# Causal masks and their identity in rounded fp32 instead of bf16, in a hybrid attention and state-space block on one core

## The chip, the cores and the metric

The program runs on one core of a Trainium2 chip. The metric is the device time of one execution in microseconds (us). TensorE is called PE here, and its weight loads, which overlap with its matmuls, are counted apart as PEld; DVE is VectorE, ACT is ScalarE, POOL is GpSimd and SP is SyncE.

## What is computed

One layer of a streaming encoder over 256 tokens of width 2048, in fp32. The part that matters here is the mixer: forgetting attention with 16 heads, and a Mamba-2 state-space mixer (SSD) with 16 heads. Both need an exponent that is cut off by a causal mask:

```python
    c = jnp.cumsum(log_f, axis=1).transpose(0, 2, 1)
    s = s + cb[..., :, None] - c[..., None, :]
    mask = k_pos[None, :] <= q_pos[:, None]
    s = jnp.where(mask[None, None], s, -jnp.inf)
    pr = jax.nn.softmax(s, axis=-1)
...
    seg = a_cum[:, :, :, None, :] - a_cum[:, :, None, :, :]
    decay = jnp.exp(jnp.where(causal[None, None, :, :, None], seg, -jnp.inf))
```

Ahead of the mixer stands the product with `w_in`. After it come `w_out`, a gated convolutional feed-forward part (`w_gate_up`, `w_down`), a gate with per-layer embeddings, and a last RMS norm.

## The kernel before

**Weights.** All weight matrices pass through a ring of four chunks of 128x1024 fp32. SP loads a chunk, ACT writes its rounded part `w_hi` (L312, fp32r, which is rounded fp32), DVE writes the rest `w_lo` (L317), and PE multiplies: hi times hi, hi times lo, lo times hi. In the front part of the kernel these are L332, L333 and L334 (128 weight columns, 256 moving columns, 8 triples to a chunk), for the value groups L372 to L374 (512 moving columns), in the feed-forward part L344 and L346.

**Order of the work.** `plan()` fixes by hand after which chunk each side step of the mixer is issued, on PE at chunk n and on ACT and DVE at chunk n + LEAD (3 later). So PE's stream is: a chunk of weights, one step of a head, a chunk of weights, and so on. The SSD heads come at about 140 to 207 us, the attention heads at about 219 to 292 us.

**The exponent of a head** is built in PSUM by `exponent_terms` (L761): one fp32r matmul with 64 rows of weights and 384 moving columns (L764) spreads a head's row of cumulated sums, `ssd_row` or `fox_row`, over the partitions. Then two matmuls (L767) with the identity `ident_bf` as weights and a mask of 128x128 as moving operand add 0 or -1e30 to the two blocks on the diagonal, at columns 0 and 256 of the bank. `ssd` calls it at L831 with `mask_s`, as the whole step of the new head behind the older head's four matmuls (L821); `fox` calls it at L811 with `mask_q`, after the older heads' transposes (L778) and products (L791) and the scores of the new head (L806, L808). The last L767 signals `e_ready` or `s_ready`: ACT's exponential L1080 waits for the first, DVE's row maximum L1425 for the second. Behind L1425 on DVE stands the scaling of the head before (L1432), and PE's transposes L778 wait for that.

**Where the masks come from.** POOL clears `ident`, four small tiles, `mask_q` and `mask_s` (L590 to L596), waits for them, and selects 1 on the diagonal of `ident` (L598). PE and ACT wait for `consts_made` at 4, which comes at L599. The masks are selected behind that (L609, L610), then two key tiles are cleared (L614), and only then are the two loads of the 16-column pieces of `w_in` issued on POOL's queue (L618, L619). DVE makes `ident_bf` from `ident` in `make_row(1)` (L1388), between the steps that make `fox_row`.

Of the kernel before, what the change touches and what calls it, by code (L numbers as in the profile page):

```python
# [26 lines left out]
F32R = mybir.dt.float32r  # L27
BF16 = mybir.dt.bfloat16
ALU = mybir.AluOpType
# [3 lines left out]
P = 128  # L33
EPS = 1e-6
MASKED = -1e30
# [10 lines left out]
def build(nc, x, p, mix_norm_w, w_in, fox_forget_bias, ssd_conv_w, ssd_conv_b, ssd_dt_bias, ssd_A_log,  # L46
          ssd_D, ssd_norm_w, w_out, ffn_norm_w, w_gate_up, ffn_conv_w, ffn_conv_b, w_down, ple_norm_w,
          w_ple_gate, w_ple_proj, final_norm_w, out):
    _, T, D = x.shape
# [73 lines left out]
    with ctx:  # L123
# [3 lines left out]
        def sem(name):  # L127
            return ctx.enter_context(nc.semaphore(name))
# [6 lines left out]
        ident = sb("ident", [P, P])  # L135
# [15 lines left out]
        def at(name, shape, dt=F32, offset=None):  # L151
            size = 4 if dt != BF16 else 2
            for n in shape[1:]:
                size *= n
            offset = top[0] if offset is None else offset
            top[0] = max(top[0], (offset + size + 31) // 32 * 32)
            assert arena + top[0] <= nc.sbuf_usable_end, (name, arena + top[0], nc.sbuf_usable_end)
            return nc.alloc_sbuf_tensor_at(name, shape, dt, offset=arena + offset)

        K1 = 1024  # L160
# [23 lines left out]
        ssd_row, fox_row = at("ssd_row", [4 * H, 3 * P], F32R), at("fox_row", [4 * H, 3 * P], F32R)  # L184
        sel = at("sel", [P, 2 * H], F32R)
        sel_f = at("sel_f", [P, 2 * H])
        ident_bf = at("ident_bf", [P, P], BF16)
        mask_q, mask_s = at("mask_q", [P, P], BF16), at("mask_s", [P, P], BF16)
        dt_tok = at("dt_tok", [P, TT, 2 * H])
        ncum_tok = at("ncum_tok", [P, TT, 2 * H])  # L190
        d_all = at("d_all", [P, H])
# [1 line left out]
        row_sum = at("row_sum", [P, H, TT])  # L193
        row_inv = at("row_inv", [P, H, TT])
        y_sum = at("y_sum", [P, T])
        y_rms = at("y_rms", [P, T])
        fdc = at("fdc", [2 * H, 4])
        xtok = at("xtok", [P, TT, D], offset=40 * K1)
        x_squares, x_ssq = at("x_squares", [P, D], offset=0), at("x_ssq", [P, TT], offset=61 * K1)
# [26 lines left out]
        ps = ctx.enter_context(nc.psum_tensor("ps", [P, 8, 512], F32))  # L226
# [20 lines left out]
        pool_step, consts_made, masks_made = sem("pool_step"), sem("consts_made"), sem("masks_made")  # L247
# [326 lines left out]
        @block.gpsimd  # L574
        def _(pool):
            steps = [0]

            def link(ins):
                steps[0] += 1
                ins.then_inc(pool_step, 1)  # L580

            def linked():
                pool.wait_ge(pool_step, steps[0])

            def select(dst, src, keep, fill, base, per_partition, per_column, n):
                return pool.affine_select(out=dst, in_=src, compare_op=keep, fill=fill, base=base,
                                          pattern=[[per_column, n]], channel_multiplier=per_partition)

            pool.memset(fdc[:, 2:3], 0.0).then_inc(consts_made, 1)
            link(pool.memset(ident[:, :], 0.0))  # L590
            link(pool.memset(sel_f[:, :], 0.0))
            link(pool.memset(fdc[:, 1:2], -1.0))
            link(pool.memset(fdw[:, 0, :], 1.0))
            link(pool.memset(mask_q[:, :], 0.0))
            link(pool.memset(mask_s[:, :], 0.0))
            pool.memset(eps[:, :], EPS).then_inc(consts_made, 1)  # L596
            linked()
            select(ident[:, :], ident[:, :], ALU.not_equal, 1.0, 0, 1, -1, P).then_inc(consts_made, 1)  # L598
            pool.memset(ones[:, :], 1.0).then_inc(consts_made, 1)  # L599

            link(select(sel_f[:, :], sel_f[:, :], ALU.not_equal, 1.0, 0, 1, -1, 2 * H))
            linked()
            select(sel_f[:, :], sel_f[:, :], ALU.not_equal, 1.0, -2 * H, 1, -1, 2 * H).then_inc(masks_made, 1)

            select(fdc[:, 1:2], fdc[:, 1:2], ALU.is_ge, 1.0, H - 1, -1, 0, 1).then_inc(masks_made, 1)

            select(fdw[:, 0, P:P + 1], fdw[:, 0, P:P + 1], ALU.is_ge, 0.0, H - 1, -1, 0, 1).then_inc(masks_made, 1)

            select(mask_q[:, :], mask_q[:, :], ALU.is_ge, MASKED, 0, 1, -1, P).then_inc(masks_made, 1)  # L609
            select(mask_s[:, :], mask_s[:, :], ALU.is_ge, MASKED, 0, -1, 1, P).then_inc(masks_made, 1)  # L610
            pool.wait_ge(masks_made, 5)
            for i, half in enumerate((kE[P // 2:P, :, :], kO[0:P // 2, :, :], conv_in[:, :, 0:4])):

                pool.memset(half, 0.0).then_inc(masks_made, 1)  # L614
                pool.wait_ge(masks_made, 6 + i)

            with nc.allow_non_contiguous_dma(reason="the forget and dt columns of w_in are 16 wide"):
                pool.dma_start(w_fd[:, :, 0:H], win_v[:, :, c_f:c_f + H]).then_inc(fd_landed, 16)  # L618
                pool.dma_start(w_fd[:, :, H:2 * H], win_v[:, :, c_dt:c_dt + H]).then_inc(fd_landed, 16)  # L619

            for norm in range(1, 3):
                if norm == 1:

                    pool.wait_ge(a_exp, 1)
                    select(fdc[:, 3:4], fdc[:, 3:4], ALU.is_ge, 1.0, -H, 1, 0, 1).then_inc(a_ready, 1)

                    for b in range(WT // 2):
                        pool.wait_ge(gated, b // 2 + 1)
                        pair = xsT[:, 2 * b:2 * b + 2, :]
                        if b > 0:  # L630
                            linked()
                        link(pool.tensor_tensor(sq[:, :, :] if b > 0 else sumsq[:, :, :], pair, pair, ALU.mult))
                        if b > 0:
                            linked()
                            link(pool.tensor_tensor(sumsq[:, :, :], sumsq[:, :, :], sq[:, :, :], ALU.add))
                    linked()
                    pool.tensor_tensor(sumsq[:, 0, :], sumsq[:, 0, :], sumsq[:, 1, :], ALU.add).then_inc(y_squared, 1)
                for b in range(KD // 2):
                    pool.wait_ge(x_new, norm * (KD // 2) + b + 1)
                    if b == 0:  # L640
                        pool.wait_ge(y_sums_made, 1)
                        if norm > 1:
                            pool.wait_ge(sums_made, norm - 1)
                    pair = xT[:, 2 * b:2 * b + 2, :]
                    if b == 0:
                        link(pool.tensor_tensor(sumsq[:, :, :], pair, pair, ALU.mult))
                        continue
                    linked()
                    link(pool.tensor_tensor(sq[:, :, :], pair, pair, ALU.mult))
                    linked()  # L650
                    link(pool.tensor_tensor(sumsq[:, :, :], sumsq[:, :, :], sq[:, :, :], ALU.add))
                linked()
                pool.tensor_tensor(sumsq[:, 0, :], sumsq[:, 0, :], sumsq[:, 1, :], ALU.add).then_inc(squares_made, 1)
# [3 lines left out]
        def _(pe):  # L657
# [103 lines left out]
            def exponent_terms(bank, j, row, mask, start):  # L761

                both = 4 * H
                pe.matmul(ps[:, bank, 0:3 * P], sel[0:both, j:j + 1].to_broadcast([both, P]), row[:, :],  # L764
                          start=start, stop=False, skip_group_check=True)
                for dst in (0, T):
                    mm = pe.matmul(ps[:, bank, dst:dst + P], ident_bf[:, :], mask[:, :],  # L767
                                   start=False, stop=True, skip_group_check=True)
                return mm

# [169 lines left out]
            for n, (g, c) in enumerate(tail):  # L940
                i = n // GROUP
# [297 lines left out]
        def _(dve):  # L1239
# [101 lines left out]
            def link(ins):  # L1341
                fd_count[0] += 1
                ins.then_inc(fd_step, 1)
                dve.wait_ge(fd_step, fd_count[0])
# [35 lines left out]
            def make_row(attention):  # L1380
                n, c = 2 * H, fdr(1)
                src = fdw[:, 2 + 2 * attention:4 + 2 * attention, :].rearrange("h a t -> h (a t)")[:, 0:3 * P]
                if attention:

                    dst = fox_row
                    link(dve.tensor_scalar(src[:, 0:P], c[:, 0:P], -1.0, None, ALU.mult))
                    link(dve.tensor_scalar(src[:, P:3 * P], c, -1.0, None, ALU.mult))
                    dve.tensor_copy(ident_bf[:, :], ident[:, :])  # L1388
                else:


                    dst = ssd_row
                    link(dve.tensor_copy(src[:, 0:P], c[:, 0:P]))
                    link(dve.tensor_scalar(src[:, P:T], c[:, P:T], c[:, P - 1:P], None, ALU.add))
                    link(dve.tensor_copy(src[:, T:3 * P], c[:, P:T]))
                    dve.tensor_copy(sel[:, :], sel_f[:, :])
                link(dve.tensor_copy(dst[0:n, :], src))
                dve.tensor_tensor(dst[n:2 * n, :], src, dst[0:n, :], ALU.subtract).then_inc(cum_ready, 1)
# [336 lines left out]
```

## Time and profile before

| | |
|---|---|
| median of 3 runs | 1259.81 us (1259.72 to 1260.19) |
| the profiled execution | 1260.43 us, its span 1258.7 us |
| busy in the span: PE, PEld | 1245.7 us (99%), 1108.7 us (88%) |
| DVE, ACT, POOL | 856.7 us (68%), 616.9 us (49%), 60.8 us (5%) |
| mean granted clock of TensorE | 0.998 of full speed |
| moved by DMA | 226.94 MB, 180 GB/s on average |

The span goes from the first to the last instruction. A matmul's record begins where it is issued to the array and contains its way through it, so that successive records overlap: what PE's time is made of is read from start to start, not from durations.

### The profile page before, as it was taken

The numbers are of one execution on the slowest core, as the hardware profiler recorded it, in microseconds if no ns is written. First come the engines' busy times: TensorE is split into PE (matmuls) and PEld (weight loads), VectorE is DVE, ScalarE is ACT, GpSimd is POOL, SyncE is SP. The second block draws the span as 40 slices with busy tenths as digits, with TensorE's granted clock in tenths as the row PEclk, the third lists the DMA queues.
The fourth block names the chain that finished last, engine by engine and source line by source line (L and its number), as shares of the span: only waits on it lengthen the run. The fifth ranks groups of instructions, "written<-read, shape, count | busy, mean of one in ns | idle before, by whom it ended". The sixth has DMA issues, their size and how long they took to land.

```text
span 1258.7 us, 21432 instructions
## 1 busy us (share of the span) xinstructions
PE 1245.7 (99%) x7838; PEld 1108.7 (88%) x7838; DVE 856.7 (68%) x1120; ACT 616.9 (49%) x810; POOL 60.8 (5%) x66
## 2 busy tenths in 40 slices
PE   8999999999999999999999999999999999999997
PEld 7999998789999888888888888888888888888885
DVE  6698777677678776767767677676746464646554
ACT  6544555656444454444444454454444344444555
POOL 2000000001213100000000000000001010101000
PEclk9999999999999999999999999999999999999999
DMA  8566555344656666666666666666665656566652
GB/s 256 168 183 184 157 146 155 114 114 125 199 172 203 186 193 186 185 196 183 191 193 185 194 187 187 194 187 188 191 190 166 216 160 217 164 212 202 198 185 101
DMA packets 165885, 226.94 MB, mean 180 GB/s; under 512 B 10209, under 2 KB 101381, under 8 KB 165701
## 3 DMA queue, kind: packets, MB, share of 16 engines
q1 hardware_dynamic: 165732, 225.90, 59.3%
q8 instruction: 38, 0.62, 0.2%
q0 software_dynamic: 96, 0.26, 0.1%
q14 instruction: 19, 0.15, 0.0%
HBM read 224.03 MB, written 2.10 MB: 180 GB/s over the span
## 4 chain that ended last, share of the span: by engine, by line
PE 97%; DVE 1%; DMA 1%; ACT 0%; SPq 0%; issue 0%; ACTq 0%; DVEq 0%
PE ps L344 39%; PE ps L346 19%; PE ps L332 8%; PE ps L333 8%; PE ps L334 8%; PE ps L372 4%; PE ps L374 4%; PE ps L373 3%; DMA w_raw<-in_w_in 1%; PE ps L764 1%; PE ps L767 1%; PE ps L808 1%; DVE h_parts L1243 0%; PE ps L791 0%; PE ps L821 0%; PE ps L778 0%
## 5 line engine op out<-in xcount | busy, mean ns | idle before, releaser
L317 DVE TENSOR_TENSOR w_lo<-w_raw,w_hi 128x1024 fp32r<-128x1024 f32 x413 | 505.9, 1230 | 318.2 <-ACT w_hi L312 317.5
L312 ACT ACTIVATE w_hi<-w_raw 128x1024 fp32r<-128x1024 f32 x413 | 435.9, 1059 | 459.4 <-PE ps L346 341.2
L344 PE MATMUL ps<-h_parts,w_hi 128*128 128x512 f32 x1408 | 488.6, 394 | 0.0
L346 PE MATMUL ps<-h_parts,w_lo 128*128 128x256 f32 x1408 | 390.2, 277 | 0.0
L344 PEld LDWEIGHTS ps<-h_parts,w_hi 128*128 128x128 f32 x1408 | 264.0, 188 | 61.5
L346 PEld LDWEIGHTS ps<-h_parts,w_lo 128*128 128x128 f32 x1408 | 264.2, 188 | 0.0
L344 PE MATMUL ps<-act_parts,w_hi 128*128 (+1 forms) x704 | 244.4, 392 | 0.0
L346 PE MATMUL ps<-act_parts,w_lo 128*128 (+1 forms) x704 | 196.8, 280 | 0.0
L332 PE MATMUL ps<-h_parts,w_hi 128*128 128x256 f32 x576 | 165.8, 288 | 0.6 <-DVE w_lo L317 0.6
L333 PE MATMUL ps<-h_parts,w_hi 128*128 128x256 f32 x576 | 162.9, 283 | 0.0
L334 PE MATMUL ps<-h_parts,w_lo 128*128 128x256 f32 x576 | 162.9, 283 | 0.0
L344 PEld LDWEIGHTS ps<-act_parts,w_hi 128*128 128x128 f32 x704 | 132.1, 188 | 29.5 <-issue 0.4
L346 PEld LDWEIGHTS ps<-act_parts,w_lo 128*128 128x128 f32 x704 | 132.2, 188 | 0.0
L332 PEld LDWEIGHTS ps<-h_parts,w_hi 128*128 128x128 f32 x576 | 110.2, 191 | 1.4 <-issue 1.3
L333 PEld LDWEIGHTS ps<-h_parts,w_hi 128*128 128x128 f32 x576 | 110.4, 192 | 0.0
L334 PEld LDWEIGHTS ps<-h_parts,w_lo 128*128 128x128 f32 x576 | 110.2, 191 | 0.0
L332 PE MATMUL ps<-mixHi,w_hi 128*128 128x256 f32 x256 | 71.8, 280 | 0.0
L334 PE MATMUL ps<-mixHi,w_lo 128*128 128x256 f32 x256 | 71.6, 280 | 0.0
L333 PE MATMUL ps<-mixLo,w_hi 128*128 128x256 f32 x256 | 71.6, 280 | 0.0
L372 PE MATMUL ps<-w_hi,h_parts 128*128 128x512 f32 x168 | 67.0, 399 | 0.6 <-DVE w_lo L317 0.6
L374 PE MATMUL ps<-w_hi,h_parts 128*128 128x512 f32 x168 | 65.8, 392 | 0.0
L373 PE MATMUL ps<-w_lo,h_parts 128*128 128x512 f32 x168 | 65.4, 389 | 0.0
(248 smaller groups left out, 1115.3 us busy)
## 6 DMA issues: line engine op xcount, KB each, us to landing
w_raw<-in_w_gate_up SPq DMA_DIRECT2D x352, 256.0 KB, 3.2
w_raw<-in_w_in SPq DMA_DIRECT2D x88, 512.0 KB, 3.7
w_raw<-in_w_down SPq DMA_DIRECT2D x88, 512.0 KB, 4.6
w_raw<-in_w_out SPq DMA_DIRECT2D x32, 512.0 KB, 4.6
w_raw<-in_w_ple_gate SPq DMA_DIRECT2D x32, 512.0 KB, 4.6
w_raw<-in_w_ple_proj SPq DMA_DIRECT2D x4, 512.0 KB, 5.3
out_x<-out_tok SPq DMA_DIRECT2D x8, 256.0 KB, 2.9
xtok<-in_x SPq DMA_DIRECT2D x3, 512.0 KB, 9.1
```

The lines of the kernel that those rows point to most:

```text
L312: act.activation(parts(n)[0], w_raw[:, n % RING, :], ACT.Copy).then_inc(w_hi_made, 1)
L317: dve.tensor_tensor(lo, w_raw[:, n % RING, :], hi, ALU.subtract).then_inc(w_lo_made, 1)
L332: pe.matmul(dst, hi, opHi(k), start=start and m % 2 == 0, stop=False, skip_group_check=True)
L333: pe.matmul(dst, hi, opLo(k), start=False, stop=False, skip_group_check=True)
L334: mm = pe.matmul(dst, lo, opHi(k), start=False, stop=stop, skip_group_check=True)
L344: pe.matmul(ps[:, bank_of[m], :], hi, both.rearrange("p b t -> p (b t)"), start=first and k == 0, stop=False, skip_group_check=True)
L346: mm = pe.matmul(ps[:, bank_of[m], T:2 * T], lo, both[:, 0, :], start=False, stop=last and k == 1, skip_group_check=True)
L372: pe.matmul(dst, a, hi, start=first and kk == 0, stop=False)
L373: pe.matmul(dst, a, lo, start=False, stop=False)
L374: mm = pe.matmul(dst, b, hi, start=False, stop=last and kk == 1)
L764: pe.matmul(ps[:, bank, 0:3 * P], sel[0:both, j:j + 1].to_broadcast([both, P]), row[:, :], start=start, stop=False, skip_group_check=True)
L767: mm = pe.matmul(ps[:, bank, dst:dst + P], ident_bf[:, :], mask[:, :], start=False, stop=True, skip_group_check=True)
```

## The change

`ident_bf`, `mask_q` and `mask_s` are no longer bf16 but fp32r, and the identity is now called `ident_r`. An fp32r tile is written rounded, so POOL makes the masks in two fp32 tiles, `mask_qf` and `mask_sf`, which lie in bytes 30 K to 31 K of the arena (where `y_part` lies later), and DVE copies both into the fp32r tiles in `make_row(1)`, right behind the identity. The three tiles grow by 256 bytes each per partition. `y_rms` gets the memory of `y_sum`. The two matmuls L767 stay as they are, but for the type of their operands.

```diff
-        ident_bf = at("ident_bf", [P, P], BF16)
-        mask_q, mask_s = at("mask_q", [P, P], BF16), at("mask_s", [P, P], BF16)
+        ident_r = at("ident_r", [P, P], F32R)
+        mask_q, mask_s = at("mask_q", [P, P], F32R), at("mask_s", [P, P], F32R)
+        mask_qf, mask_sf = (at(n, [P, P], offset=30 * K1 + 512 * i) for i, n in enumerate(("mask_qf", "mask_sf")))
...
-        y_rms = at("y_rms", [P, T])
+        y_rms = y_sum
...
-            link(pool.memset(mask_q[:, :], 0.0))
-            link(pool.memset(mask_s[:, :], 0.0))
+            link(pool.memset(mask_qf[:, :], 0.0))
+            link(pool.memset(mask_sf[:, :], 0.0))
...
-            select(mask_q[:, :], mask_q[:, :], ALU.is_ge, MASKED, 0, 1, -1, P).then_inc(masks_made, 1)
-            select(mask_s[:, :], mask_s[:, :], ALU.is_ge, MASKED, 0, -1, 1, P).then_inc(masks_made, 1)
+            select(mask_qf[:, :], mask_qf[:, :], ALU.is_ge, MASKED, 0, 1, -1, P).then_inc(masks_made, 1)
+            select(mask_sf[:, :], mask_sf[:, :], ALU.is_ge, MASKED, 0, -1, 1, P).then_inc(masks_made, 1)
...
                 for dst in (0, T):
-                    mm = pe.matmul(ps[:, bank, dst:dst + P], ident_bf[:, :], mask[:, :],
+                    mm = pe.matmul(ps[:, bank, dst:dst + P], ident_r[:, :], mask[:, :],
                                    start=False, stop=True, skip_group_check=True)
...
-                    dve.tensor_copy(ident_bf[:, :], ident[:, :])
+                    dve.tensor_copy(ident_r[:, :], ident[:, :])
+                    for mask, values in ((mask_q, mask_qf), (mask_s, mask_sf)):
+                        dve.tensor_copy(mask[:, :], values[:, :])
```

## Rows read from the trace of the kernel before

**Rows 1.** The page's chain that ended last, by engine.

```profile
PE 97%; DVE 1%; DMA 1%; ACT 0%; SPq 0%; issue 0%; ACTq 0%; DVEq 0%
```

**Rows 2.** Busy time by stretch (window, its length, busy time with count per engine).

```profile
138.00:208.00 70.00, 70.00 (x526) 63.15 (x525) 56.87 (x88) 43.42 (x82) 0.00 (x0) 1.00 0.51 146
218.00:293.00 75.00, 75.00 (x476) 61.56 (x475) 51.13 (x123) 43.08 (x111) 0.00 (x0) 1.00 0.40 115
```

**Rows 3.** Line L767: ns min/median/max, first and last start in us.

```profile
L767 PEld LDWEIGHTS ps<-mask_s,ident_bf x32: 96/98/99, 140.5 to 206.4; 128*128 128x128 bf16 x32
...
L767 PE MATMUL ps<-mask_q,ident_bf x32: 219/224/230, 219.5 to 291.1; 128*128 128x128 bf16 x32
```

**Rows 4.** Timeline of one SSD head, PE (start us, us; x2 starts merged).

```profile
151.13 0.34 PE L821 MATMUL ps<-probT_lo,xdt_parts 128*64 128x256 f32 x2
151.40 0.44 PE L764 MATMUL ps<-ssd_row,sel 64*128 64x384 f32 x1
151.77 0.28 PE L767 MATMUL ps<-mask_s,ident_bf 128*128 128x128 bf16 x2
...
152.06 0.28 PE L333 MATMUL ps<-h_parts,w_hi 128*128 128x256 f32 x1
```

**Rows 5.** The same head, weight loads.

```profile
151.76 0.11 PEld L767 LDWEIGHTS ps<-mask_s,ident_bf 128*128 128x128 bf16 x2 [0.19 <-issue]
...
151.95 0.19 PEld L333 LDWEIGHTS ps<-h_parts,w_hi 128*128 128x128 f32 x1
```

**Rows 6.** Timeline of one attention head, PE and PEld.

```profile
256.82 0.11 PEld L767 LDWEIGHTS ps<-mask_q,ident_bf 128*128 128x128 bf16 x2 [0.19 <-issue]
...
257.24 0.39 PE L373 MATMUL ps<-w_lo,h_parts 128*128 128x512 f32 x1
```

**Rows 7.** Groups by line and shape: fp32r weight load, fp32r matmul of 128 columns (mean ns).

```profile
L344 PEld LDWEIGHTS ps<-h_parts,w_hi 128*128 128x128 f32 x1408 | 264.0, 188 | 61.5
...
L821 PE MATMUL ps<-probT_hi,xdt_parts 128*128 128x128 f32 x16 | 3.5, 221 | 0.0
```

**Rows 8.** Timeline around the 32-row fp32 transposes L745, PE and PEld.

```profile
75.90 0.28 PE L334 MATMUL ps<-h_parts,w_lo 128*128 128x256 f32 x1
76.11 0.43 PE L745 MATMUL ps<-ident,fdw 32*128 32x32 f32 x4
...
76.47 0.19 PEld L332 LDWEIGHTS ps<-h_parts,w_hi 128*128 128x128 f32 x1
76.58 0.19 PEld L333 LDWEIGHTS ps<-h_parts,w_hi 128*128 128x128 f32 x1
76.70 0.19 PEld L334 LDWEIGHTS ps<-h_parts,w_lo 128*128 128x128 f32 x1
```

**Rows 9.** Timeline of the start: fp32 transposes, then bf16 weight loads.

```profile
7.53 0.66 PE L679 MATMUL ps<-ident,xtok 128*128 128x128 f32 x4 [0.98 <-DMA xtok<-in_x]
...
7.92 0.42 PEld L661 LDWEIGHTS ps<-idle_in 128*128 128x128 bf16 x3
```

**Rows 10.** Timeline of one attention head: DVE, and the next head's first weight load.

```profile
257.15 0.62 DVE L1425 TENSOR_REDUCE neg_max<-ps 128x1 f32<-128x128 f32 x2 [1.03 <-PE ps L767]
...
257.88 0.55 DVE L1432 TENSOR_SCALAR prob<-prob,row_inv 128x128 f32<-128x128 f32 x2
...
259.55 0.49 PEld L778 LDWEIGHTS ps<-ident,prob 128*128 128x128 f32 x3
```

**Rows 11.** Timeline of DVE, the copy of the identity.

```profile
88.41 0.23 DVE L1388 CAST ident_bf<-ident 128x128 bf16<-128x128 f32 x1
```

**Rows 12.** Groups by line up to 90.73 us, the end of a `w_lo` behind it.

```profile
L332 PE MATMUL ps<-h_parts,w_hi 128*128 128x256 f32 x200 | 57.4, 287 | 0.6 <-DVE w_lo L317 0.6
...
L317 DVE TENSOR_TENSOR w_lo<-w_raw,w_hi 128x1024 fp32r<-128x1024 f32 x27 | 32.6, 1222 | 6.6 <-ACT w_hi L312 6.5
```

**Rows 13.** Timeline of POOL at the start.

```profile
0.85 0.20 POOL L590 MEMSET ident<- 128x128 f32 x1
...
1.34 0.20 POOL L594 MEMSET mask_q<- 128x128 bf16 x1
```

## The prediction

> **What bounds the kernel now.** I read the chain of waits first: 97% of what ended last is PE [rows 1]. Then the stretches in which the change does its work: in the 70 us of the SSD heads and in the 75 us of the attention heads PE is busy all the time, at full granted clock, while DVE and ACT have idle time [rows 2]. So PE's stream is the bound there, and what is added to or taken from it from start to start comes out at the end of the kernel one for one. Everything else that the change touches has to be shown to be late enough to matter.
>
> **The matmuls L767.** There are 32 heads, two mask matmuls each. The type changes nothing in what moves: a bf16 mask matmul is recorded with 224 ns [rows 3], an fp32r matmul of the same 128 columns with 221 ns [rows 7]. What changes is the weight load: 98 ns in bf16 [rows 3] against 188 ns for 128x128 in fp32r [rows 7]. Durations overlap, so I take the price from starts.
>
> Now, in the SSD head, the first mask load begins at 151.76 and the load of L333, the second of the next chunk, at 151.95 [rows 5]; L333's matmul begins at 152.06 [rows 4]. That is 0.30 us for two mask loads, the load of L332 and the load of L333. How fp32r loads follow each other when nothing hides the first is seen behind the transposes L745: loads at 76.47, 76.58 and 76.70 [rows 8], so 0.11 to 0.12 us from one to the next. A mask matmul has only 128 columns and can't hide a load of that length, so the sequence is bound by loads. With fp32r masks: first mask load 0, second 0.11, L332's 0.22, L333's 0.33 to 0.34, and L333's matmul another 0.11 to 0.12 behind its load, at 0.45. The difference to 0.30 is 0.15 us a head. In the attention heads the same stretch is 0.42 us now, from 256.82 to L373 at 257.24, as L372 moves 512 columns [rows 6]; the two mask loads stand ahead of it just as before and are lengthened by the same 0.15. The sum is 32 x 0.15 = 4.8 us. With 0.14 to 0.16 a head, which is what two decimals leave open, it is 4.5 to 5.1.
>
> No row shows fp32r loads around two matmuls of 128 columns, so I bound the price further out. From below: the wait ahead of the first mask load (next part) might swallow one of the two longer loads, which leaves one difference of the records, 188 - 98 = 90 ns, and 2.9 us in all. From above: each 128-column matmul might not hide any of the following load; 128 columns take half of the 0.12 step of 256 columns, so 2 x 0.06 more, 0.27 us a head and 8.6 us. I take 4.8, because rows 8 are the nearest: the same type, the same load size, on the same engine directly behind a wait of the same kind.
>
> **The wait ahead of the masks stays.** L764 begins at 151.40 and the first mask load only at 151.76, 0.08 before the end of L764's record; it was not prefetched [rows 4, 5]. If that came from the change of type, from fp32r to bf16, the change would remove it. The rows speak against it. L764 itself follows the fp32r matmuls L821 with no change of type, and starts 0.07 before the end of their record (151.47), also unprefetched [rows 4]. Going from 128 to 32 rows at 76.11 and back at 76.47, again 0.07 before the end of what ran (76.18 and 76.54), is the same [rows 8]. And a bf16 load at 7.92 begins 0.27 before the end of the fp32 transposes that run (8.19), so prefetched [rows 9]. The number of weight rows, 64 against 128, explains all four; the type explains none. I keep the wait, and its price is in both kernels.
>
> **What waits for the masks.** The signal comes about 0.15 us later. In attention, DVE's maximum L1425 waits for it now already; behind it on DVE stand the scaling L1432, done at 258.43, and PE's transposes need that at 259.55 [rows 10]. That is 1.1 us of slack. Both ends of it move by the same 0.15, since PE reaches the transposes later too; even if they didn't, it would take 0.15 of 1.1. ACT's exponentials of the SSD heads are consumed a whole head later. Cost nothing; if this cover were gone, 0.15 a head more.
>
> **DVE's copies.** One copy of 128x128 costs 0.23 us now [rows 11]. Written in fp32r it has twice the bytes; two more are added, so 0.5 us, or 0.7 if each took half as long again, once, at 88.4 us. Up to 90.73 DVE has finished 27 chunks of `w_lo`, and PE has begun 200 / 8 = 25 [rows 12], where a chunk is 24 steps of 0.12 or 2.9 us. So DVE is more than one chunk ahead, and 0.7 us is hidden. With no cover it would be 0.7 us once.
>
> **POOL.** Clearing 128x128 takes 0.20 us in fp32 and in bf16 [rows 13], so the identity, for which PE and ACT wait at the start, is as early as before; the selects come behind it. Nothing here; no more than a few tenths if a wider tile were slower. `y_rms` on `y_sum`, and tiles that move by some hundred bytes: no instruction is added, no wait either. Nothing.
>
> **Sum.** The profiled execution took 1260.43 us, so 1265.2 for it; that is 0.6 above the median of 1259.81, and against the median I predict 1259.8 + 4.8 = 1264.6 us. About 0.2% (2.5 us) is what a measurement of this kernel can tell from no change.
>
> **Rivals.** (1) Fp32r weights load as fast as bf16 ones. Then the cost is 0, 1259.8 us. Against it stands every 128x128 fp32r load, 188 ns over 1408 records [rows 7]; for it, only that none of them loads the identity. Chance 0.04. The Trainium skill, "TensorE: Matmul & The Clock Gate", section on weight-path perf modes, says that Fast Weight Load is on for 128 weights whose type is not FP32 and measures it at about 2 times. If fp32r counted as not FP32, the page would give this rival; by 98 against 188 ns the trace says that it counts as FP32.
>
> (2) Not slower: the wait ahead of the masks does hang on fp32r followed by bf16, a pair of types that occurs nowhere else, and goes. L764's columns would end about 0.27 us after its start (a load of 0.11 and 384 columns, three times 0.06), so the mask matmul could start there instead of after 0.37, and its 0.11 load would be hidden. That gives back 0.10 + 0.11 = 0.21 against a cost of 0.15: 0.06 a head or 1.9 us, so 1257.9 us. It decides once the first mask matmul can go ahead more than 0.15 us earlier than now. For it: this wait sits exactly at the change of type, 32 times. Against it: the three other waits and the one free passage above. Chance 0.05.
>
> (3) Fp32r at 128 columns next to such loads runs slower than I take it, or loads aren't hidden at all: the upper end, 8.6 us, 1268.4 us. Against it: 221 ns for that very shape [rows 7]. Chance 0.05.
>
> (4) A smaller cost than one load per matmul, 2.9 us or less, as bounded above: 1262.7 us. Chance 0.08, half of it still above 0.2%.
>
> The forecast itself, 4.5 to 5.1 us, with what the overlap at the edges may add or take, 1263.8 to 1265.4, has the rest, 0.78. For the range I go down to the lower bound, 1262.7, and up to 1266.6, half way to case 3, which leaves out some 0.15. Slower by over 0.2%: 0.78 + 0.05 + 0.04 plus a little of case 1 being only partly true, 0.88. Within 0.2%: cases 1, 2 (1.9 us is inside) and half of 4, 0.11. Faster: 0.01, for a case 2 that gives back more.
>
> **What the profile after would show.** L767's loads at about 185 to 190 ns instead of 98, its matmuls still about 221 ns. From the first mask load to L333's matmul 0.45 us instead of 0.30, to L373's 0.57 instead of 0.42. The first mask load still 0.36 to 0.37 after L764. Two more copies on DVE near 88.5 us, and no PE wait for `w_lo` there. The stages before 140 us and after 293 us as long as before, each of the two head stages longer by 2.4 us. If the first mask load moves towards L764, case 2 is right; if L767's loads stay near 98 ns, case 1; if its matmuls grow well past 221 ns, case 3.

## The result, and the profile after

The changed kernel takes 1264.55 us (median of 7 runs, 1264.22 to 1265.62) against 1260.04 us for the kernel before (7 runs, 1259.72 to 1260.92): 4.5 us slower, ratio 1.0036, 95% interval 1.0026 to 1.0046. Forecast was 4.8 us slower, within 1262.7 to 1266.6.

One line was added above them, so L764 and L767 of the kernel before are L765 and L768 now, and L332 to L334 are L333 to L335. The first fence is the changed kernel's view of line L768 (ns min/median/max, first and last start), against [rows 3].

```profile
L768 PEld LDWEIGHTS ps<-mask_s,ident_r x32: 186/188/190, 140.0 to 208.2; 128*128 128x128 f32 x32
L768 PE MATMUL ps<-mask_s,ident_r x32: 272/302/330, 140.0 to 208.2; 128*128 128x128 f32 x32
```

The weight loads are 188 ns long instead of 98, as forecast. The matmuls' records grew from 224 to 302 ns, which was not forecast; what that means is told in the part on the prediction. Next, the timeline of one SSD head of the changed kernel, PE and then PEld (start us, us), against [rows 4, 5]:

```profile
151.04 0.34 PE L822 MATMUL ps<-probT_lo,xdt_parts 128*64 128x256 f32 x2
151.31 0.44 PE L765 MATMUL ps<-ssd_row,sel 64*128 64x384 f32 x1
151.67 0.44 PE L768 MATMUL ps<-mask_s,ident_r 128*128 128x128 f32 x2
151.95 0.33 PE L333 MATMUL ps<-h_parts,w_hi 128*128 128x256 f32 x1
152.12 0.28 PE L334 MATMUL ps<-h_parts,w_hi 128*128 128x256 f32 x1
...
151.67 0.30 PEld L768 LDWEIGHTS ps<-mask_s,ident_r 128*128 128x128 f32 x2 [0.19 <-issue]
151.89 0.19 PEld L333 LDWEIGHTS ps<-h_parts,w_hi 128*128 128x128 f32 x1
152.00 0.19 PEld L334 LDWEIGHTS ps<-h_parts,w_hi 128*128 128x128 f32 x1
```

From the first mask load at 151.67 to the second matmul of the next chunk at 152.12 it is 0.45 us; before it was 0.30 [rows 4, 5]. The two mask loads last 0.30 together, so the second starts at about 151.78, and the next two follow at 151.89 and 152.00: a chain of loads, 0.11 us apart. The wait of 0.36 from L765 to the first mask load is unchanged. In attention the same stretch goes from 0.42 [rows 6] to 0.56, from 259.69 to 260.25:

```profile
259.69 0.30 PEld L768 LDWEIGHTS ps<-mask_q,ident_r 128*128 128x128 f32 x2 [0.19 <-issue]
...
260.25 0.39 PE L374 MATMUL ps<-w_lo,h_parts 128*128 128x512 f32 x1
```

Whether that happens in all 32 heads is read from the spreading matmul, which each head has once. Its first and last starts, kernel before and then the changed kernel:

```profile
L764 PE MATMUL ps<-ssd_row,sel x16: 435/438/438, 140.2 to 206.0; 64*128 64x384 f32 x16
L764 PE MATMUL ps<-fox_row,sel x16: 435/438/443, 219.2 to 290.7; 64*128 64x384 f32 x16
```

```profile
L765 PE MATMUL ps<-ssd_row,sel x16: 435/438/439, 139.7 to 207.7; 64*128 64x384 f32 x16
L765 PE MATMUL ps<-fox_row,sel x16: 435/438/443, 221.0 to 294.6; 64*128 64x384 f32 x16
```

From the first SSD head to the last it is 68.0 us instead of 65.8, in attention 73.6 instead of 71.5. That is 2.2 and 2.1 us for 15 heads each, so 0.14 to 0.15 a head, or 4.6 us for 32. Nothing is added between the two stages (13.3 against 13.2). From the last head to the end it is 968 us in both. The first head comes 0.5 us earlier in this one execution (139.7 against 140.2 us), and that is why the span is only 4.1 us longer (1262.8 against 1258.7). That start moves from trace to trace, 139.6 to 141.1 us over all the runs below, with no order by type; why stays open.

DVE's copies, near 88 us, against [rows 11]:

```profile
87.88 0.23 DVE L1389 CAST ident_r<-ident 128x128 fp32r<-128x128 f32 x1
88.02 0.22 DVE L1391 CAST mask_q<-mask_qf 128x128 fp32r<-128x128 f32 x1
88.15 0.22 DVE L1391 CAST mask_s<-mask_sf 128x128 fp32r<-128x128 f32 x1
88.29 0.34 DVE L1400 CAST fox_row<-fdw 32x384 fp32r<-32x384 f32 x1
```

The two more take 0.27 us (88.02 to 88.29), and the fp32r copy of the identity has the same 0.23 us as the bf16 one. POOL clears an fp32 mask in the same time as a bf16 one [rows 13]:

```profile
1.33 0.20 POOL L595 MEMSET mask_qf<- 128x128 f32 x1
```

### The profile page after: what moved, and what is told of

Same layout as the page of the kernel before. It is cut to its first block, busy times and chain, and to the rows that moved or that the text cites. A ratio compares the mean times of both kernels' runs of the same rounds, so it can differ in the third digit from the quotient of the medians.

```text
span 1262.8 us, 21434 instructions
## 1 busy us (share of the span) xinstructions
PE 1249.2 (99%) x7838; PEld 1113.2 (88%) x7838; DVE 856.8 (68%) x1122; ACT 616.9 (49%) x810; POOL 60.7 (5%) x66
## 4 chain that ended last, share of the span: by engine, by line
PE 97%; DVE 1%; DMA 1%; ACT 0%; SPq 0%; issue 0%; ACTq 0%; DVEq 0%
PE ps L345 39%; PE ps L347 19%; PE ps L333 8%; PE ps L334 8%; PE ps L335 8%; PE ps L373 4%; PE ps L375 3%; PE ps L374 3%; DMA w_raw<-in_w_in 1%; PE ps L768 1%; PE ps L765 1%; PE ps L809 1%; DVE h_parts L1244 0%; PE ps L792 0%; PE ps L822 0%; PE ps L779 0%
## 5 line engine op out<-in xcount | busy, mean ns | idle before, releaser
L333 PE MATMUL ps<-h_parts,w_hi 128*128 128x256 f32 x576 | 165.2, 287 | 0.9 <-DVE w_lo L318 0.9
L334 PE MATMUL ps<-h_parts,w_hi 128*128 128x256 f32 x576 | 162.9, 283 | 0.0
L335 PE MATMUL ps<-h_parts,w_lo 128*128 128x256 f32 x576 | 162.9, 283 | 0.0
L333 PEld LDWEIGHTS ps<-h_parts,w_hi 128*128 128x128 f32 x576 | 110.3, 191 | 1.8 <-issue 1.6
L334 PEld LDWEIGHTS ps<-h_parts,w_hi 128*128 128x128 f32 x576 | 110.4, 192 | 0.0
L335 PEld LDWEIGHTS ps<-h_parts,w_lo 128*128 128x128 f32 x576 | 110.2, 191 | 0.0
L333 PE MATMUL ps<-mixHi,w_hi 128*128 128x256 f32 x256 | 71.8, 280 | 0.0
L335 PE MATMUL ps<-mixHi,w_lo 128*128 128x256 f32 x256 | 71.6, 280 | 0.0
L334 PE MATMUL ps<-mixLo,w_hi 128*128 128x256 f32 x256 | 71.6, 280 | 0.0
L375 PE MATMUL ps<-w_hi,h_parts 128*128 128x512 f32 x168 | 65.8, 391 | 0.0
```

The source lines that it names most:

```text
L333: pe.matmul(dst, hi, opHi(k), start=start and m % 2 == 0, stop=False, skip_group_check=True)
L334: pe.matmul(dst, hi, opLo(k), start=False, stop=False, skip_group_check=True)
L335: mm = pe.matmul(dst, lo, opHi(k), start=False, stop=stop, skip_group_check=True)
L375: mm = pe.matmul(dst, b, hi, start=False, stop=last and kk == 1)
```

## The experiments

All ratios are to the kernel before, run on the same chip beside each experiment. The changed kernel was not run again beside them: where a time is compared with it, its 1264.55 us is meant, and the kernel before lay within 0.3 us in all comparisons (1259.96 to 1260.27).

### The rest of the change alone

The changed kernel with the three tiles in bf16 again. POOL's fp32 masks, DVE's two more copies and the shared `y_rms` stay.

```diff
-        ident_r = at("ident_r", [P, P], F32R)
-        mask_q, mask_s = at("mask_q", [P, P], F32R), at("mask_s", [P, P], F32R)
+        ident_r = at("ident_r", [P, P], BF16)
+        mask_q, mask_s = at("mask_q", [P, P], BF16), at("mask_s", [P, P], BF16)
```

> Everything of the change but the type of the matmul operands: POOL makes both masks in fp32, DVE makes three copies, now into bf16 tiles, and y_rms lies on y_sum. Theory (all of the cost is in PE's weight loads): no difference to the kernel before, ratio 1.0000 within 0.0005. Rival (part of the 4.5 us comes from POOL's fp32 work at the start or DVE's two more copies): 0.3 to 1 us more than before, ratio up to 1.0008.

1260.01 us against 1260.05, ratio 0.9999 (0.9990 to 1.0007). The cost hangs on the type of the matmul's operands. What the rest of the change may cost is at most 0.9 us by the interval, and nothing by the trace: from the first head to the last the two stages take 65.8 and 71.6 us, in the kernel before 65.8 and 71.5.

### Only one of the two stages

The changed kernel with `mask_s` and a second identity in bf16; attention keeps fp32r.

```diff
+        ident_bf = at("ident_bf", [P, P], BF16)
-        mask_q, mask_s = at("mask_q", [P, P], F32R), at("mask_s", [P, P], F32R)
+        mask_q, mask_s = at("mask_q", [P, P], F32R), at("mask_s", [P, P], BF16)
...
-                    mm = pe.matmul(ps[:, bank, dst:dst + P], ident_r[:, :], mask[:, :],
+                    mm = pe.matmul(ps[:, bank, dst:dst + P], (ident_bf if mask is mask_s else ident_r)[:, :], mask[:, :],
...
+                    dve.tensor_copy(ident_bf[:, :], ident[:, :])
```

> The changed kernel with the SSD heads' mask and the identity that adds it back in bf16; attention keeps fp32r. Theory (two longer weight loads in each of 32 heads, 0.146 us a head in the trace of the changed kernel): half the cost, 16 x 0.146 = 2.3 us over the kernel before, so a ratio of about 1.0019, with the stretch from the first mask load to the second matmul of the next chunk at 0.30 us in the SSD heads and 0.45 us in attention. Rival (the cost sits in one of the two stages, for instance where DVE waits for the masks): either 0 or the whole 4.7 us.

1262.28 us against 1260.05, ratio 1.0018 (1.0009 to 1.0027): 2.2 us, half of the cost. The trace has it where it should be: from the first SSD head to the last 65.9 us, where the kernel before has 65.8, and in attention 73.6, as the changed kernel has. The cost goes by heads, and it does not matter that in attention DVE waits for the masks and in the SSD stage ACT does. (The 0.45 us expected for the attention heads was a slip; the stretch is 0.56 there, as in the changed kernel.)

### Twice as many mask matmuls

Each mask added twice, once to the changed kernel and once to the kernel before.

```diff
-                for dst in (0, T):
+                for dst in (0, T, 0, T):
```

> The changed kernel with each mask added twice (four mask matmuls a head instead of two; a masked score is then -2e30, and the exponential of it is still 0). Theory (each fp32r mask matmul costs one weight load step of about 0.11 us): 32 x 2 x 0.11 = 7.0 us over the changed kernel, 11.6 over the kernel before, ratio 1.0092. Rival (the fp32r cost is a fixed one at the border to the neighbours, and inside a run of mask matmuls only the 128 columns count, 0.055 to 0.06 us each): 3.5 to 3.8 us over the changed kernel, ratio 1.0065.

> The kernel before with each mask added twice (four bf16 mask matmuls a head). Theory (a bf16 load is short enough to hide behind 128 columns; the step is the 0.06 us from one mask matmul's start to the next): 32 x 2 x 0.06 = 3.8 us over the kernel before, ratio 1.0030. Rival (the type makes no difference to the step, only to the border): the same increase as the fp32r kernel with four mask matmuls has over the changed kernel.

With fp32r 1271.95 us, ratio 1.0091 (1.0077 to 1.0106), 7.4 us over the changed kernel; with bf16 1263.58 us, ratio 1.0027 (1.0016 to 1.0037), 3.5 us over the kernel before. Divided by the 64 matmuls added, a mask matmul costs 0.116 us in fp32r and 0.055 in bf16. The weight loads of one head, fp32r and then bf16, with the matmul that follows the four (start us, us; four loads merged):

```profile
152.80 0.52 PEld L768 LDWEIGHTS ps<-mask_s,ident_r 128*128 128x128 f32 x4 [0.19 <-issue]
153.24 0.19 PEld L333 LDWEIGHTS ps<-h_parts,w_hi 128*128 128x128 f32 x1
```

```profile
151.84 0.23 PEld L767 LDWEIGHTS ps<-mask_s,ident_bf 128*128 128x128 bf16 x4 [0.19 <-issue]
152.03 0.19 PEld L332 LDWEIGHTS ps<-h_parts,w_hi 128*128 128x128 f32 x1
```

Four fp32r loads and the way to the next take 0.44 us, 0.11 each; four bf16 ones 0.19. The rival, a fixed price at the border, is out: within a run of equal matmuls the weight loads set the time in fp32r, while the 0.055 us of bf16 is the time of 128 columns (a 256-column matmul steps by 0.12). The Trainium skill, "TensorE: Matmul & The Clock Gate", section on LDWEIGHTS, gives a load's time in ns as its columns divided by 1.2; for 128 columns that is an estimate of 107 ns. The 0.11 us from one fp32r load to the next agrees with it; the 188 ns of a load's record do not.

### The spreading matmul on 128 rows

Does the wait ahead of the masks come from the rows or from the types? The spreading matmul L764 gets all 128 rows, the upper 64 zero in weights and moving tile, once with fp32r masks (the changed kernel) and once with bf16 masks (the kernel before). Two instructions on DVE clear the rows.

```diff
-        ssd_row, fox_row = at("ssd_row", [4 * H, 3 * P], F32R), at("fox_row", [4 * H, 3 * P], F32R)
+        ssd_row, fox_row = at("ssd_row", [P, 3 * P], F32R), at("fox_row", [P, 3 * P], F32R)
...
-                pe.matmul(ps[:, bank, 0:3 * P], sel[0:both, j:j + 1].to_broadcast([both, P]), row[:, :],
+                pe.matmul(ps[:, bank, 0:3 * P], sel[:, j:j + 1].to_broadcast([P, P]), row[:, :],
...
+                dve.tensor_scalar(dst[2 * n:P, :], kE[P // 2:P, 0:2, :].rearrange("p a t -> p (a t)")[:, 0:3 * P], 0.0, None, ALU.mult)
                 link(dve.tensor_copy(dst[0:n, :], src))
```

> The changed kernel with the spreading matmul ahead of the masks on all 128 rows instead of 64 (rows 64 to 127 of its weights and of the moving tile are zero, so the sums are the same); DVE clears those rows once. Theory (the waits ahead of this matmul and ahead of the first mask load come from the change of the number of rows, 64 against 128): both go. From L821's last matmul to this one 0.15 becomes 0.06, and from it to the first mask matmul 0.37 becomes 0.16 to 0.18. That is 0.28 a head or 9 us under the changed kernel; about 1255.5 us, ratio to the kernel before 0.9965. Rival (the waits come from something else, such as the one-column weights that are broadcast, or from a fixed order of the loads): nothing changes, ratio 1.0036.

> The kernel before (bf16 masks) with the spreading matmul on all 128 rows, the unused ones zero. Theory (number of rows alone): both waits go here too, and the first bf16 mask load is issued well before the spreading matmul's record ends; 9 us under the kernel before, ratio 0.993, and 4 to 5 us faster than the fp32r kernel with 128 rows. Rival (a change from fp32r to bf16 has a wait of its own, hidden until now under that of the rows; this is the prediction's case 2): only the wait ahead of the spreading matmul goes, the 0.37 us to the first mask matmul stays; 32 x 0.09 to 0.24 = 3 to 5 us under the kernel before, and the bf16 kernel is not faster than the fp32r one with 128 rows.

With fp32r masks 1252.99 us, ratio 0.9943 (0.9929 to 0.9956); with bf16 masks 1252.01 us, ratio 0.9940 (0.9926 to 0.9953), both against 1260.27. The wait belongs to the change from 64 rows to 128. The gain is 11.6 us for the changed kernel, where 9 was expected, and 8.3 us for the kernel before. One SSD head with fp32r masks, PE and PEld:

```profile
146.56 0.39 PE L764 MATMUL ps<-ssd_row,sel 128*128 128x384 f32 x1
146.79 0.33 PE L767 MATMUL ps<-mask_s,ident_r 128*128 128x128 f32 x2
146.96 0.33 PE L333 MATMUL ps<-h_parts,w_hi 128*128 128x256 f32 x1
147.13 0.28 PE L334 MATMUL ps<-h_parts,w_hi 128*128 128x256 f32 x1
...
146.62 0.36 PEld L767 LDWEIGHTS ps<-mask_s,ident_r 128*128 128x128 f32 x2
```

And with bf16 masks, where L332 and L333 are the chunk's first two:

```profile
146.59 0.39 PE L763 MATMUL ps<-ssd_row,sel 128*128 128x384 f32 x1
146.82 0.29 PE L766 MATMUL ps<-mask_s,ident_bf 128*128 128x128 bf16 x2
...
147.12 0.28 PE L333 MATMUL ps<-h_parts,w_hi 128*128 128x256 f32 x1
...
146.82 0.11 PEld L766 LDWEIGHTS ps<-mask_s,ident_bf 128*128 128x128 bf16 x2
146.89 0.19 PEld L332 LDWEIGHTS ps<-h_parts,w_hi 128*128 128x128 f32 x1
```

Two things are to be seen. First, with 128 rows the first fp32r mask load starts at 146.62, 0.06 after the spreading matmul, and runs beside its columns. From the mask matmuls to the second matmul of the chunk it is now 0.34 (146.79 to 147.13) instead of 0.45 (151.67 to 152.12): one of the two longer loads no longer costs anything. That is 32 x 0.11 = 3.5 of the 11.6 us, and the other 8.1 are the waits themselves, as many as the bf16 kernel gained. Second, the bf16 load does not run beside those columns. It starts at 146.82, 0.23 after the spreading matmul, about when its columns have ended. So here a bf16 load behind an fp32r matmul does have a wait of its own, which lay hidden under the wait for the rows. It costs little here, since a bf16 load is short. The gap between the types shrinks to 1.0 us. The two intervals can't tell that from zero, but the traces agree with it: from the spreading matmul to the second matmul of the chunk 0.57 us in fp32r and 0.53 in bf16, and 32 x 0.04 = 1.3. For bf16 neither the expectation came true (a mask load well ahead of the columns' end, 4 to 5 us faster than fp32r) nor its rival (3 to 5 us gained, and not faster than fp32r).

In the attention heads the two waits shrink at another place. Here is one with fp32r masks, from the second L808 on, and then the same two records of the bf16 kernel:

```profile
255.25 0.38 PE L808 MATMUL ps<-kO,qT 128*128 128x256 f32 x1
255.27 0.52 PE L764 MATMUL ps<-fox_row,sel 128*128 128x384 f32 x1
255.64 0.33 PE L767 MATMUL ps<-mask_q,ident_r 128*128 128x128 f32 x2
...
255.46 0.36 PEld L767 LDWEIGHTS ps<-mask_q,ident_r 128*128 128x128 f32 x2
```

```profile
254.51 0.52 PE L763 MATMUL ps<-fox_row,sel 128*128 128x384 f32 x1
...
254.88 0.11 PEld L766 LDWEIGHTS ps<-mask_q,ident_bf 128*128 128x128 bf16 x2 [0.20 <-issue]
```

From the spreading matmul to the first mask matmul it is still 0.37 us, as with 64 rows. What is gone is the 0.31 ahead of the spreading matmul (259.01 to 259.32 in the changed kernel), now 0.02: it is issued at once, and its record holds the time that it waits for what runs before it. So the 0.37 from start to start doesn't say here that a wait for the rows is left; by that step alone the rival, under which it stays, would seem true. The order of the loads is that of the SSD head: the fp32r load starts 0.18 before the mask matmul, which is the time of 384 columns at 0.12 per 256, and the bf16 load only with the mask matmul. From the first spreading matmul to the last, over 15 heads each, the SSD stage goes from 65.8 to 62.5 us in bf16 and attention from 71.5 to 67.2; in fp32r it is 68.0 to 63.0 and 73.6 to 67.7. For 32 heads that makes 8.1 and 11.6 us, where 8.3 and 11.6 were measured.

### One mask matmul instead of two

One load of the identity, the mask read twice, 256 moving columns written in two pieces; for the changed kernel and for the kernel before.

```diff
-                for dst in (0, T):
-                    mm = pe.matmul(ps[:, bank, dst:dst + P], ident_r[:, :], mask[:, :],
-                                   start=False, stop=True, skip_group_check=True)
-                return mm
+                return pe.matmul(ps[:, bank, :].rearrange("p (a t) -> p a t", a=2)[:, :, 0:P], ident_r[:, :],
+                                 mask[:, :].unsqueeze(1).to_broadcast([P, 2, P]),
+                                 start=False, stop=True, skip_group_check=True)
```

> The changed kernel with both mask blocks added by one matmul: one load of the identity, the mask read twice as 256 moving columns, written to columns 0 to 127 and 256 to 383. Theory (bound by weight loads, 0.11 each): one load less and the 256 columns take about one load's time, so the stretch from the first mask load to the second matmul of the next chunk goes from 0.45 to about 0.34, 3.5 us under the changed kernel, ratio to the kernel before about 1.0009. Rival (columns bound it, or a moving operand read twice or an output in two pieces is slower): no gain, ratio 1.0036 or more.

> The kernel before with both mask blocks added by one bf16 matmul, as in the fp32r kernel with one. Theory (bf16 loads are short, so columns bound it, and there are 256 either way): nearly no change, ratio 0.999 to 1.0005, and the two types differ by less than 0.06 us a head (2 us) once there is one load only. Rival (a fixed price per mask matmul of any type): a gain as large as the fp32r kernel's, 3.5 us.

With fp32r 1261.50 us, ratio 1.0011 (1.0002 to 1.0020), 3.1 us under the changed kernel, as expected from one load less. With bf16 1258.37 us, ratio 0.9984 (0.9974 to 0.9993): 1.9 us gained where next to nothing was expected (1.3 at most), and the types are still 3.1 us apart instead of under 2. What my expectation missed is the load that comes next. Here is the bf16 kernel with one mask matmul, the mask's load and L332's, and the matmuls:

```profile
151.78 0.28 PE L766 MATMUL ps<-mask_s,ident_bf 128*128 128x256 bf16 x1
...
152.02 0.29 PE L333 MATMUL ps<-h_parts,w_hi 128*128 128x256 f32 x1
...
151.77 0.10 PEld L766 LDWEIGHTS ps<-mask_s,ident_bf 128*128 128x128 bf16 x1 [0.19 <-issue]
151.78 0.20 PEld L332 LDWEIGHTS ps<-h_parts,w_hi 128*128 128x128 f32 x1
```

L332's load starts 0.01 us behind the mask's, and the 256 columns of the mask run beside it. So in bf16 the first mask matmul of the kernel before was free as to columns, and the second one cost its 0.055 us: 32 x 0.055 = 1.8 us, the gain measured. In fp32r the one load left still stands alone behind the wait for the rows, 0.11 us in each head. That is 3.5 us by the starts, against the 3.1 measured.

### Both edits together

128 rows and one mask matmul, in fp32r and in bf16; the two diffs above together.

> The changed kernel with both: the spreading matmul on 128 rows and one mask matmul of 256 columns. Theory as the runs so far leave it (an fp32r load costs its 0.11 us only where it can't run beside the columns of the matmul before it; with 128 rows it can, and 256 columns hide the next load too): from the spreading matmul to the mask 0.23, to the next chunk's first matmul 0.12, to its second 0.12, so 0.46 in the SSD heads against 0.57 with 128 rows and two mask matmuls; 3.3 us under that kernel, 1249.7 us, ratio to the kernel before 0.992. Rival (each fp32r load has a price of its own that nothing hides, or the gains of the two edits overlap): 1252 us or more, ratio 0.9935 or more.

> The kernel before with both edits, masks in bf16. Theory (behind fp32r columns a bf16 load starts only when the columns have ended, and the fp32r load behind a bf16 matmul stays exposed): from the spreading matmul to the mask 0.23, then 0.04 and 0.20, 0.47 in the SSD heads; 1.8 us under the bf16 kernel with 128 rows and two mask matmuls, 1250.2 us, ratio 0.9925. So the fp32r kernel with both edits is as fast as this one or up to 0.5 us faster. Rival (bf16 loads are simply the shorter ones and win by a constant of at least 1 us): this one is faster than the fp32r one by 1 us or more.

With fp32r 1250.29 us, ratio 0.9921 (0.9908 to 0.9935); with bf16 1250.86 us, ratio 0.9924 (0.9911 to 0.9938), against 1259.96. The types come out equal within what these runs can tell, with nothing seen of the 4.5 us, and both are faster than the kernel before by 9 to 10 us. One SSD head, fp32r and then bf16:

```profile
151.37 0.39 PE L764 MATMUL ps<-ssd_row,sel 128*128 128x384 f32 x1
151.60 0.28 PE L766 MATMUL ps<-mask_s,ident_r 128*128 128x256 f32 x1
151.72 0.28 PE L333 MATMUL ps<-h_parts,w_hi 128*128 128x256 f32 x1
151.84 0.27 PE L334 MATMUL ps<-h_parts,w_hi 128*128 128x256 f32 x1
```

```profile
150.89 0.39 PE L763 MATMUL ps<-ssd_row,sel 128*128 128x384 f32 x1
151.12 0.28 PE L765 MATMUL ps<-mask_s,ident_bf 128*128 128x256 bf16 x1
151.16 0.36 PE L332 MATMUL ps<-h_parts,w_hi 128*128 128x256 f32 x1
151.36 0.28 PE L333 MATMUL ps<-h_parts,w_hi 128*128 128x256 f32 x1
```

Both take 0.47 us from the spreading matmul to the chunk's second matmul. In fp32r the steps are 0.23, 0.12 and 0.12. The last two are columns alone, and the mask's load is hidden as well:

```profile
151.32 0.19 PEld L764 LDWEIGHTS ps<-ssd_row,sel 128*128 128x128 f32 x1
151.43 0.19 PEld L766 LDWEIGHTS ps<-mask_s,ident_r 128*128 128x128 f32 x1
```

The 0.23 are 0.05 more than 384 columns (0.18): the spreading matmul's own load, 0.11 long, starts only 0.05 ahead of it. That half of a load is left exposed in both types. In bf16 the steps are 0.23, 0.04 and 0.20: the fp32r load behind the mask is exposed instead. The rival, that bf16 wins by 1 us or more, is not excluded by the two times, each of which is known to 1.7 us; the traces exclude it. From the first spreading matmul to the last it is 61.6 us in the SSD stage and 66.5 in attention in fp32r, 61.8 and 66.5 in bf16.

## Why the prediction was right

**PE is the bound, one for one: right.** 4.3 us more from start to start on PE for 30 heads, so 4.6 for 32, and 4.5 at the end.

**Two longer loads per head, 0.15 us: right.** The traces give 0.14 to 0.15, and the four loads start where the prediction put them: at 0, 0.11, 0.22 and 0.33, the matmul at 0.45. The price came from the row nearest in kind, fp32r loads directly behind a wait [rows 8]. The upper bound, loads not hidden at all, and the lower one, one load swallowed by the wait, both missed. What the lower bound supposes, one load hidden, does happen once the wait is gone, with 128 rows; but the types are then 1.0 us apart and not 2.9, as the bf16 load comes late.

**The wait stays and comes from the rows: right in the verdict, incomplete in the reason.** The experiments with 128 rows show that the rows cause it. But "the type explains none" was too strong. The row on which it leaned, a bf16 load issued beside fp32 transposes [rows 9], does not carry over to fp32r: there the bf16 load came only with the end of the columns, at 0.23 us. Case 2 was right that this pair has a wait, and wrong that it sets the time while the rows' wait is longer.

**What waits for the masks, DVE's copies, POOL: right.** The copies and POOL cost nothing that shows, as the kernel with the rest of the change alone has it; the two more copies took 0.27 us where 0.5 was reckoned. That kernel says nothing of the later signal, since its masks are bf16. For the signal it is the changed kernel's trace: PE is busy throughout both head stages, and they are longer by the price of the loads and no more.

**The marker for case 3 was wrong.** The mask matmuls' records did grow well past 221 ns, to 302, while case 3 did not occur. Here the matmul's record contains the time that it waits for its own weights: the two together are 0.44 us long in the changed kernel, and 0.33 with 128 rows, where the first mask's weights were there. The 221 ns [rows 7] belong to a matmul with its weights at hand. Starts, not durations, told the cost.

## What to carry to other kernels

A small matmul cost here the longer of its columns and its weight load, and where a wait stood ahead of it, its load as well. The fp32r identity nearly doubled the recorded load, and that was paid only where the load couldn't run beside earlier columns. Before trading types, look for what keeps loads from being prefetched: here 32 small matmuls on 64 rows instead of 128 cost 8 us, nearly twice what the type did. Where two matmuls share their weights, one with both pieces as moving columns does the work of both, 3.1 us cheaper here in fp32r and 1.9 in bf16.

## What was not expected of the hardware

A matmul on half the rows, among others on 128, is dearer than one on all of them. Changing the weight rows from 128 to 64 and back stopped the prefetching of loads both times. Filling the unused rows with zeros took 8.3 us off the kernel with bf16 masks and 11.6 off the one with fp32r, 0.26 and 0.36 us a head. Loads on 64 or 32 rows between others on 128, and the loads on 128 behind them, wait until 0.07 to 0.08 us before the running matmul's record ends [rows 4, 5, 8]. Not every other number of rows does it. The same trace has three transposes on 96, 92 and 88 rows, and these are prefetched:

```profile
39.33 0.28 PE L334 MATMUL ps<-h_parts,w_lo 128*128 128x256 f32 x1
39.45 0.41 PE L697 MATMUL ps<-ident,par_rows 96*128 96x96 f32 x3
...
39.35 0.33 PEld L697 LDWEIGHTS ps<-ident,par_rows 96*128 96x128 f32 x3
39.62 0.19 PEld L332 LDWEIGHTS ps<-h_parts,w_hi 128*128 128x128 f32 x1
```

Their first load starts at 39.35, 0.26 before the record of L334 ends, and L332's, back on 128 rows, at 39.62, 0.24 before theirs ends. So the prediction's "number of weight rows" holds for 64 and 32 against 128, and not for 88 to 96. The Trainium skill, "TensorE: Matmul & The Clock Gate", section on the mechanism of packing small matmuls, says that a weight load overlaps with running matmuls only when its row group differs. These traces go against that "only": fp32r loads on the same 128 rows as the running matmul are prefetched, one every 0.12 us with 256 columns. They don't test the other half, as no matmul here runs on rows that its neighbour leaves free.

A bf16 load behind an fp32r matmul of 384 columns started 0.23 us after it, an fp32r load in the same place 0.06 us after it; in the attention heads it was 0.37 and 0.19. Why is open: behind fp32 transposes a bf16 load did start early [rows 9], and no run took the length of the load and its type apart, or put another matmul ahead of it.
